# A hybrid decoder layer on one core: three more products in high and low parts, four page buffers, and the sample values loaded later

## What is computed

```python
h = rmsnorm(x, norm_mix);  proj = h @ w_in            # width 1024 -> conv, q, k/v, gates
conv_in = concat(conv_prev, cc * chh)                 # short convolution over 3 tokens
y_conv = (cb * conv(conv_in, conv_w)) @ w_out_conv
o = g0*compressed(qn) + g1*selected(qr) + g2*window(qr)    # sparse attention, three branches
y_nsa = o @ w_out_nsa
x = x + (sig(mg0) * y_conv + sig(mg1) * y_nsa) @ w_o  # merge output
h2 = rmsnorm(x, norm_ffn);  q = h2 @ peer_wq          # expert queries, top 16 of 128 x 128
y = x + sum_k softmax(top)_k * gelu(h2 . u_k) * v_k   # all 16384 experts as dense tiles here
```

## Time and profile before

| | us |
|---|---|
| median of the three timed runs | 1330.59 |
| profiled execution, its own time | 1331.84 |
| its span | 1330.2 |
| TensorE busy | 1306.4 (98%) |
| VectorE busy | 796.4 (60%) |
| ScalarE busy | 600.2 (45%) |
| GpSimd busy | 236.9 (18%) |
| mean granted clock of TensorE | 0.989 |

### The profile page before, as it was taken

One profiled execution on the slowest core, in us unless ns is written; L12 is line 12 of the kernel. 1 busy time (PEld: TensorE's weight loads), 2 busy tenths in 40 slices (PEclk: granted clock), 3 DMA queues, 4 the chain that ended last, 5 costly groups with the idle time before them and its releaser, 6 DMA issues.

```text
span 1330.2 us, 24262 instructions
## 1 busy us (share of the span) xinstructions
PE 1306.4 (98%) x9199; PEld 1226.9 (92%) x9199; DVE 796.4 (60%) x1398; ACT 600.2 (45%) x1178; POOL 236.9 (18%) x243
## 2 busy tenths in 40 slices
PE   7999999999999999999999999999999999999998
PEld 5687877877789999999999999999999999999998
DVE  5443137664475999966667777765545445444544
ACT  5222223221143544457777777764444444444442
POOL 3330454220000598970000000000000000000000
PEclk8999989999999999999999999999999999999999
DMA  7677347453465345454333444335555455555553
GB/s 290 197 214 81 99 135 257 138 169 121 156 207 171 104 151 177 148 163 135 127 130 130 133 130 130 128 127 166 204 162 171 160 172 161 169 163 167 166 166 107
DMA packets 75186, 208.99 MB, mean 157 GB/s; under 512 B 15040, under 2 KB 27008, under 8 KB 74368
## 3 DMA queue, kind: packets, MB, share of 16 engines
q1 hardware_dynamic: 61344, 186.25, 43.4%
q0 software_dynamic: 6464, 17.81, 4.3%
q10 hardware_dynamic: 7264, 3.40, 1.2%
HBM read 204.14 MB, written 7.44 MB: 159 GB/s over the span
## 4 chain that ended last, share of the span: by engine, by line
PE 94%; POOL 2%; issue 1%; DVE 1%; ACT 1%; DMA 0%; DVEq 0%; SPq 0%; ACTq 0%
PE ps L1630 21%; PE ps L1705 20%; PE ps L1252 13%; PE ps L1635 10%; PE ps L1712 10%; PE ps L1680 5%; PE ps L1362 5%; POOL w_lo L442 2%; PE ps L1272 2%; PE ps L1497 1%; PE ps L1461 1%; PE ps L1279 1%; PE ps L1656 1%; PE ps L1493 1%; PE ps L1286 0%
## 5 line engine op out<-in xcount | busy, mean ns | idle before, releaser
L703 ACT ACTIVATE w_hi<-ring 128x1024 fp32r<-128x1024 f32 x272 | 288.6, 1061 | 394.8 <-PE ps L1705 223.2
L1088 DVE TENSOR_TENSOR w_lo<-ring,w_hi 128x1024 fp32r<-128x1024 f32 x224 | 274.2, 1225 | 296.8 <-ACT w_hi L703 296.8
L1630 PE MATMUL ps<-h_hi,w_hi 128*128 128x288 f32 x1024 | 284.1, 303 | 0.0
L1630 PE MATMUL ps<-h_lo,w_hi 128*128 128x288 f32 x1024 | 279.1, 297 | 0.0
L1630 PEld LDWEIGHTS ps<-h_hi,w_hi 128*128 128x128 f32 x1024 | 192.8, 188 | 0.2 <-issue 0.2
L1630 PEld LDWEIGHTS ps<-h_lo,w_hi 128*128 128x128 f32 x1024 | 192.7, 188 | 0.0
L442 POOL TENSOR_TENSOR w_lo<-ring,w_hi 128x1024 fp32r<-128x1024 f32 x48 | 133.4, 2791 | 174.9 <-ACT w_hi L703 174.6
L1635 PE MATMUL ps<-h_hi,w_lo 128*128 128x288 f32 x1024 | 156.6, 295 | 2.0 <-POOL w_lo L442 1.8
L1635 PEld LDWEIGHTS ps<-h_hi,w_lo 128*128 128x128 f32 x1024 | 143.9, 188 | 3.0 <-POOL w_lo L442 3.0
L1705 PE MATMUL ps<-h_hi,w_hi 128*128 128x288 f32 x1024 | 146.1, 295 | 0.0
L1705 PEld LDWEIGHTS ps<-h_hi,w_hi 128*128 128x128 f32 x1024 | 139.1, 188 | 0.0
(11 more groups left out here) (293 smaller groups left out, 1714.5 us busy)
## 6 DMA issues: line engine op xcount, KB each, us to landing
ring<-in_uT SPq DMA_DIRECT2D x128, 512.0 KB, 3.3
ring<-in_v SPq DMA_DIRECT2D x128, 512.0 KB, 3.3
ring<-in_wout SPq DMA_DIRECT2D x32, 512.0 KB, 3.3
ring<-in_wT SPq DMA_DIRECT2D x28, 512.0 KB, 4.3
ring<-in_wtok SPq DMA_DIRECT2D x8, 512.0 KB, 4.4
arena<-in_cache_slc_v POOLq DMA_DIRECT2D x64, 64.0 KB, 2.4
arena<-in_cache_cmp_k POOLq DMA_DIRECT2D x32, 64.0 KB, 3.0
arena<-in_w SPq DMA_DIRECT2D x1, 2048.0 KB, 11.3
```

Source lines behind the costliest of these rows:

```text
L703: act.activation(w_hi[e % 2][:, :], ring[:, (W_Q + e) % RING, :], ACT.Copy).then_inc(S["w_high"], 1)
L1088: dve.tensor_tensor(w_lo[e % 2][:, :], ring[:, (W_Q + e) % RING, :], w_hi[e % 2][:, :].bitcast(F32), ALU.subtract)\
L1630: last = pe.matmul(ps[:, bank, 0:NT], w_hi[e % 2][:, k * P:(k + 1) * P], mov[:, k, :], start=(k == 0 and mov is mov_hi), stop=False, skip_ ...
```

## The change

Convolution, attention output and merge output are done in three passes as well. For this x (times norm_mix, before the division by the root) is split in all 288 columns, not 256, and the convolution takes the unnormalised parts, so VectorE multiplies by the norm's factor afterwards: cc by its square (`r_sq`, in place of ScalarE's copy), z by itself. ScalarE makes the high parts of the 24 tiles (tok_high(12) to (23) inside the head rows' work, w_high(0) to (11) later) and of the attention and merge results (o_high, m_high); GpSimd makes the low parts of the weights (conv_low, POOL_LOW), VectorE those of the results (o_low, m_low). Page buffers go from five to four, the fourth in the place where sample values lie later, so chunks 3 and 4 are SyncE's, chunk 5 comes behind GpSimd's convolution subtractions, and the values of set 0 are loaded only when the compression is done. Half of set 1's values moves to SyncE. The wait for h_ready moves to behind the compression.

```diff
-XCS = 5
+XCS = 4
+XC_SEM = [(0, 1), (1, 1), (2, 1), (3, 1), (4, 1), (0, 2), (2, 2), (1, 2)]
...
+E_O, E_Q = W_O - W_YN, W_Q - W_YN
+E_U = E_Q + Q_TILES
+E_V = E_U + U_TILES
+POOL_LOW = [*range(E_Q), *range(E_Q + 18, E_U + ROUTE_AT + 2)]
...
-        x_hi = h2_hi[:, :, 0:SEQ]
...
+        x_hi = m_hi = h2_hi
...
-              [ar("a", 4096 + 2048 * i, 2048) for i in range(3)] + [xc_more[:, 2048 * i:2048 * i + 2048] for i in range(2)]]
+              [ar("a", 4096 + 2048 * i, 2048) for i in range(3)] + [ar("vset", KC * NT, 2048)]]
+        r_sq = ar("b", 6216, NT)
...
-            if 3 <= i < XCS:
-                eng.wait_ge(S["slots_used"], W_CONV)
             if i >= XCS:
                 eng.wait_ge(S["comp_mm"], mm_count(PAGED[i - XCS]))
...
+                before = i - RING
+                if before >= W_YN:
+                    low_done(sp, before - W_YN)
+                elif before >= W_MG:
+                    sp.wait_ge(S["slots_used"], used(before))
+                elif before >= W_CONV:
+                    sp.wait_ge(S["tok_lo_used"], before + 1)
+                elif before >= 0:
+                    sp.wait_ge(S["slots_used"], before + 1)
...
-                if i < W_CONV + 4:
-                    load_chunks(sp, 2, range(4 * (i - W_CONV), 4 * (i - W_CONV) + 4))
-                if W_CONV + 4 <= i < W_CONV + 8:
-                    load_chunks(sp, 4, range(4 * (i - W_CONV - 4), 4 * (i - W_CONV - 4) + 4))
-                if i == W_CONV + 8:
+                if i < W_MG:
+                    which = (i - W_CONV) // 4
+                    load_chunks(sp, 2 + which, range(4 * ((i - W_CONV) % 4), 4 * ((i - W_CONV) % 4) + 4))
+                if i == W_MG:
+                    load_chunks(sp, 6)
+                if i == W_MG + 1:
                     load_keys(sp, 0, 1)
                     load_keys(sp, 0, 2)
-                if i == W_MG:
-                    load_chunks(sp, 6)
                 if i == W_MG + RING:
                     load_keys(sp, 2, 1)
                     load_keys(sp, 2, 2)
+                if W_MG + RING < i <= W_MG + RING + 6:
+                    n = i - W_MG - RING - 1
+                    load_values(sp, 1, 2 + n // 3, range(3 * (n % 3), 3 * (n % 3) + 3))
...
+            load_chunks(pool, 0)
+            load_chunks(pool, 1)
+            for e in range(W_CONV, W_MG):
+                pool.wait_ge(S["tok_high"], e + 1)
+                pool.wait_ge(S["tok_lo_used"], e - 1)
+                pool.tensor_tensor(w_lo[e % 2][:, :], ring[:, e % RING, :], w_hi[e % 2][:, :].bitcast(F32), ALU.subtract)\
+                    .then_inc(S["conv_low"], 1)
+            load_chunks(pool, 5)
+            load_chunks(pool, 7)
             load_keys(pool, 0, 0)
-            load_values(0)
...
             pool.wait_ge(S["comp_mm"], 10)
-            load_values(1)
-            for b in (2, 1, 3, 4, 5, 6, 7):
+            for b4 in range(SETB):
+                load_values(pool, 0, b4, range(PAGES + 1))
+            load_keys(pool, 2, 0)
+            for b4 in range(2):
+                load_values(pool, 1, b4, range(PAGES + 1))
+            for b in (1, 3, 4, 5, 6, 7):
                 load_keys(pool, b, 0)
             pool.wait_ge(S["win_kept"], 32)
...
-                act.activation(x_hi[:, k, :], xT[:, k, 0:SEQ], ACT.Copy, scale=M("norm_mix")[:, k:k + 1]).then_inc(S["x_high"], 1)
+                act.activation(x_hi[:, k, :], xT[:, k, :], ACT.Copy, scale=M("norm_mix")[:, k:k + 1]).then_inc(S["x_high"], 1)
...
+                    if e < W_CONV + 2:
+                        act.wait_ge(S["tok_low"], e - 1)
+                    else:
+                        act.wait_ge(S["conv_low"], e - 1 - W_CONV)
...
             copy_samples(1)
+            tok_high(12)
             copy_quarters(2)
+            tok_high(13)
             copy_tokens(2, 0)
             copy_tokens(2, 1)
...
-            def copy_cc(c):
-                act.wait_ge(S["slots_used"], W_CONV + 3 * c + 1)
-                if c:
-                    act.wait_ge(S["u_ready"], c)
-                act.activation(rr[:, 1, :], ps[:, 5, 0:NT], ACT.Copy).then_inc(S["cc_copied"], 1)
...
                 act.wait_ge(S["qk_var"], t + 1)
                 act.activation(st[0:n, 16:28], st[0:n, 0:12], ACT.Sqrt).then_inc(S["qk_std"], 1)
+                tok_high(W_CONV + 3 * t + 2)
...
-                copy_cc(t)
+                tok_high(W_CONV + 3 * t + 3)
                 act.wait_ge(S["qk_ready"], t + 1)
...
                         act.dma_start(O[["wk", "wv"][v]][:, WINDOW - NQ:WINDOW, :], src).then_inc(done, 16)
+                tok_high(W_CONV + 3 * t + 4)
 
                 act.wait_ge(S["qk_turned"], t + 1)
...
+            def o_high(columns):
+
+                act.activation(o_hi[:, :, columns], oT[:, :, columns], ACT.Copy).then_inc(S["o_high"], 1)
+
+            act.wait_ge(S["po_copied"], 4)
+            o_high(slice(0, SEQ))
+            w_high(0)
+            copy_weights(1)
+            w_high(1)
+            copy_values(1)
+            copy_heads(1)
+            act.wait_ge(S["so_copied"], 2)
+            o_high(slice(SEQ, NT))
+
+            def m_high(m):
+
+                act.wait_ge(S["merged"], m + 1)
+                act.activation(m_hi[:, m, :], mg[:, m, :], ACT.Copy).then_inc(S["m_high"], 1)
+
+            for j in range(4):
+                m_high(2 * j)
+                w_high(j + 2)
+                m_high(2 * j + 1)
             for k in range(KC):
+                w_high(E_O + k + 2)
                 act.wait_ge(S["x1_ready"], k + 1)
                 act.activation(xsq2[:, k, :], xT[:, k, :], ACT.Square).then_inc(S["x_squared"], 1)
                 act.wait_ge(S["hg_ready"], k + 1)
                 act.activation(hg_hi[:, k, :], hg[:, k, :], ACT.Copy).then_inc(S["hg_high"], 1)
-                if k == KC - 2:
-                    w_high(0)
...
+                dve.wait_ge(S["tok_lo_used"], W_CONV + 3 * c + 1)
+                dve.tensor_tensor(rr[:, 1, :], ps[:, 5, 0:NT], r_sq, ALU.mult).then_inc(S["cc_copied"], 1)
                 dve.wait_ge(S["cc_copied"], c + 1)
-                dve.wait_ge(S["slots_used"], W_CONV + 3 * c + 2)
+                dve.wait_ge(S["tok_lo_used"], W_CONV + 3 * c + 2)
...
+                link(dve.tensor_tensor(zT[:, c, :], zT[:, c, :], rr[:, 0, :], ALU.mult))
+                dve.wait_ge(S["tok_lo_used"], W_CONV + 3 * c + 3)
...
+            def o_low(columns, count):
+
+                dve.wait_ge(S["o_high"], count)
+                dve.tensor_tensor(o_lo[:, :, columns], oT[:, :, columns], o_hi[:, :, columns].bitcast(F32), ALU.subtract).then_inc(S["o_low"], 1)
...
             gate_conv((4, 5))
             gate(15)
+            o_low(slice(0, SEQ), 1)
             gate_conv((6, 7))
+            o_low(slice(SEQ, NT), 2)
+
+            def m_low(m):
+
+                dve.wait_ge(S["m_high"], m + 1)
+                dve.tensor_tensor(m_lo[:, m, :], mg[:, m, :], m_hi[:, m, :].bitcast(F32), ALU.subtract).then_inc(S["m_low"], 1)
...
                     dve.wait_ge(S["merged"], m)
                 link(dve.tensor_tensor(mt, ps[:, 4 + m % 2, 0:NT], mg[:, 8 + m, :], ALU.mult))
                 dve.tensor_tensor(mg[:, m, :], mg[:, m, :], mt, ALU.add).then_inc(S["merged"], 1)
+                if m:
+                    m_low(m - 1)
+            m_low(KC - 1)
...
+            def conv_product(i, bank):
+
+                pe.wait_ge(S["tok_high"], i + 1)
+                for k in range(KC):
+                    for x in (x_hi, x_lo):
+                        last = pe.matmul(ps[:, bank, 0:NT], w_hi[i % 2][:, k * P:(k + 1) * P], x[:, k, :],
+                                         start=(k == 0 and x is x_hi), stop=False, skip_group_check=True)
+                last.then_inc(S["tok_hi_used"], 1)
+                pe.wait_ge(S["conv_low"], i + 1 - W_CONV)
+                for k in range(KC):
+                    last = pe.matmul(ps[:, bank, 0:NT], w_lo[i % 2][:, k * P:(k + 1) * P], x_hi[:, k, :],
+                                     start=False, stop=(k == KC - 1), skip_group_check=True)
+                last.then_inc(S["tok_lo_used"], 1)
...
-                    pe.wait_ge(S["h_ready"], KC)
...
-                project(W_CONV + 3 * c, 5, xT).then_inc(S["slots_used"], 1)
+                conv_product(W_CONV + 3 * c, 5)
...
             pe.wait_ge(S["yc_used"], KC)
+            pe.wait_ge(S["o_high"], 2)
+            pe.wait_ge(S["o_low"], 2)
...
-                last = project(W_YN + m // 2, 4 + m % 2, oT, 4, (m % 2) * 512)
-                last.then_inc(S["slots_used" if m % 2 else "y_even"], 1)
-            pe.wait_ge(S["merged"], KC)
-            for m in range(KC):
-                if m >= 2:
-                    pe.wait_ge(S["x1_ready"], m - 1)
-                project(W_O + m, 2 + m % 2, mg).then_inc(S["slots_used"], 1)
-            def split_tile(e, bank, mov_hi, mov_lo):
...
+                last.then_inc(S["lo_used" if m % 2 else "y_even"], 1)
...
+                    if parts:
```

(36 more changed lines are left out.)

137 lines of the change are left out of this document (70 added, 67 removed).

## The result

The kernel after took 1332.80 us (median of 12 executions, 1327.31 to 1335.03), the kernel before 1327.05 beside it (12, 1324.35 to 1331.01): the ratio is 1.0032, 95% interval 1.0016 to 1.0048, some 4 us slower. Repeated beside 29 executions of before it was 1.0021 (1.0008 to 1.0034). The profiled execution has a span of 1331.3 us, only 1.1 more than before's: before's profiled execution, 1331.84, lies above the range of these twelve, after's, 1333.02, at its median. So the profiles show where work and waits are, and what they are worth has to be read from many executions.

The account below looks back on a forecast made before the run. TensorE's own work was taken as the bound (94% of the chain that ended last). Terms 0.3 - 1.1 + 1.4 + 3.0 + 1.8 = +5.4 us on 1331.84 gave 1337.2, or 1336.0 from the timed median 1330.59; range 1319 to 1343.

Parts of the forecast that it names:

- the clock's term: Falls to half clock at TensorE's idles, 1.75 us each: +1.4 us in the convolution, +1.8 in the outputs.
- the walk: Each changed stretch followed op by op in each engine's program order, with durations from the trace and hand-overs of 0.05 to 0.3 us.
- the outputs' stalls: Attention and merge output: GpSimd's subtractions and VectorE's SBUF ops delay TensorE at the crossing, loop and tail; +3.0 us.
- What a subtraction costs: GpSimd's subtraction (2.36 us a tile) and VectorE's two-SBUF-input ops shut each other out whole; the waiting one goes first.
- Convolution stage: Subtractions cut into head_rows, TensorE idles 4.6 us before round 2's transposes, stage ends at 120.2; -1.1 us where 8.2 are hoped for.
- hg's tensor_scalar: Merge output: this SBUF-to-SBUF op taken as shut out by GpSimd too; were it free, +3.0 would become -1.9.
- Moved loads: Page, key and value loads shifted between SyncE and GpSimd still arrive before use; cost nothing.
- start: Ahead of the first tiles, x split in 288 columns for 256: 8 ops on each of two engines, 0.03 longer each; +0.3 us.
- (B): Exclusion hardly bites, subtractions fall into VectorE's pauses; -13.4 us, 1317; decided if round 2's transposes start before 102; chance 0.24.
- (C): Two-input ops shut out but hg free, clock holds or falls once; -2.7 to +0.3 us, 1329; chance 0.14.
- (D): A transfer comes late, chunk 6's cover breaking once a page costs SyncE 1.5 us; +8 to +12, 1341; chance 0.08.

Follow-up runs that it names:

- the best version: The kernel after with all weight subtractions on VectorE in place of GpSimd, two of them moved behind operations TensorE waits for: 1313.09 us, ratio 0.9904.

## Why the prediction was wrong, though its total came close

The direction was right, the time 1336.0 was forecast over a median of 1330.59: +5.4 us; measured are +4.2 and +2.8 in the ratios, +5.75 and +3.85 in the medians. But that is luck: two errors cancel. The sum had +2.2 us of work and +3.2 of clock, and the executions have -4.2 of work and +7.1 of clock (the second comparison; in the first the clocks of before are not on record, after's own twelve lost 3 us more there). The step that failed in size is the clock's term, +1.4 and +1.8 for +7.1; the step that failed in the walk is the outputs' stalls, +3.0 for -0.2.

- **What a subtraction costs: right.** In the convolution stage GpSimd's took 2.4 us in the open and 5.5 for two with a wait, VectorE's products of 0.54 and 0.95 us took 2.6 and 3.05. Operations with a PSUM input ran free (L1166 stands at 0.45 us beside GpSimd's 357.84). The one that waited went first in the rows shown.
- **Convolution stage, -1.1 us: mechanism right, size off.** The idle was foretold at 4.6 us, released by head_rows' last operation, and is 3.82, with both of GpSimd's subtractions inside head_rows as walked. The transposes were walked to 72.8, 90.7 and 106.2 and came at 70.20, 88.07 and 102.98, 1.6 to 2.3 us sooner when the stage's earlier start is taken off. Measured alone the part is worth -3.7 of work.
- **Attention and merge output, +3.0: wrong.** It measured -0.2. The attention output took 14.9 us for 16.1, for in its loop only one operation for each subtraction was held up (L1151, 1.8 us); the tail took 7.0 for 7.7. Crossing and merge output came out at 32.4 for 32.2, but by two more errors that cancel: the crossing was walked with 4.3 us of idle and had 2.7, and the loop, right in every link (4.07 us for 4.3), was to bind for two or three tiles and bound for five turns.
- **hg's tensor_scalar: right.** No row had shown it; it takes 2.1 to 2.6 us for 0.37 as long as GpSimd subtracts. The Trainium skill ("SBUF — State Buffer", section "Who interferes with whom") says that tensor_scalar can enter a mode in which it and GpSimd block each other, and the trace agrees. That the loop hangs on it is shown by moving it: 3.20 us a tile.
- **Clock, +3.2: the term that failed.** It was priced at falls of 1.75 us beside the idles alone, and partly as a replacement of the one before. Measured are 3.6 for the convolution, 2.4 for the outputs, 7.1 for both. In after's profile the fall at the idle misses 3.4 us (2.4 of it behind 102.98), where the old one at 117 missed 1.8; a further one, at 138 to 146, where the walk had nothing, misses 3.35, and the next one 1.8 less than before's.
- **Moved loads, 0, and start, +0.3: right.** Measured together +0.4 of work, within 0.2% of the time; one profile of thirteen has a late key load, of 1.6 us.
- **Rivals.** (B) was to decide by transposes before 102; they start at 102.98, and 51.5 us behind the stage's start where 102 would be 49.6, and the exclusion bites. Its size is what the kernel reaches with the subtractions elsewhere: -13.4 for it, -13.6 and -15.7 of work measured. (C) needed hg to run free, and it doesn't. (D) did not occur.

**What stays open.** Five pairs of kernels differ in the idle of the convolution. Put into before it brought +6.0 us of clock, into the best version +4.4 (+3.0 to +7.4). Taking it out brought 4.3 with the outputs on GpSimd (+7.1 to +2.8), 2.1 with the outputs on VectorE (+7.7 to +5.6), and 0.6 for the convolution alone (+3.6 to +2.9); each of these is uncertain by 1.2 to 2. All have the same sign, the last two are within the scatter, and work and clock together come to 5.2 to 9.5 us. So an idle there brings a loss of clock, of a size that is not settled. Three passes seem to bring one of their own. A fall between 130 and 147 stands in 8 of 11 profiles of kernels with the convolution in three passes, also in some without the idle, and in none of the 5 with one pass (one of them with the idle put in). It takes something from the one behind it, so the whole stretch counts: from 100 to 215 us the clock misses 6.8 in each of the four profiles with one pass and no idle (8.5 with it), 8.5 to 10.3 in the four with three passes and no idle, 8.5 to 13.7 in the seven with both. That is 1.7 to 3.5 us for three passes; what sets it was not found.
